# A transformer block with sparse attention, linear attention and 32 experts: the activation stage of the expert loop re-cut, and two steps of the loop put in another order

## The reference, cut to what matters

```python
def expert_block(xb, e):
    hgu = xb @ w_gate_up[e] + b_gate_up[e]          # 1024 -> 2048
    gate, up = jnp.split(hgu, 2, axis=-1)
    gate = jnp.minimum(gate, 7.0)
    up = jnp.clip(up, -7.0, 7.0)
    act = (up + 1.0) * (gate * jax.nn.sigmoid(1.702 * gate))
    return act @ w_down[e] + b_down[e]
```

## Time and profile before

| | us |
|---|---|
| median of 3 runs (1467.7, 1471.64, 1471.86) | 1471.64 |
| the profiled execution | 1467.8 |
| its span | 1466.0 |
| PE busy | 1378.1 (94%) |
| DVE busy | 498.9 (34%) |
| ACT busy | 249.7 (17%) |
| share of the chain that ended last: PE, DMA, SP's queue, ACT | 73%, 12%, 9%, 4% |
| bytes read | 482 MB |

### The profile page before, as it was taken

How to read it: one execution, slowest core, us unless ns; L and a number is a source line. 1 busy time by engine, 2 the same in 40 slices (tenths; PEclk the granted TensorE clock), 3 DMA queues, 4 the chain that set the end, 5 groups by cost and what they waited for, 6 DMA issues and landing times.

```text
span 1466.0 us, 17062 instructions
## 1 busy us (share of the span) xinstructions
PE 1378.1 (94%) x6275; PEld 619.7 (42%) x6276; DVE 498.9 (34%) x1032; ACT 249.7 (17%) x426; POOL 10.7 (1%) x35
## 2 busy tenths in 40 slices
PE   6999999999989999999999999999999999899996
PEld 3888455888443333333333333333333333223321
DVE  2250024556543233333333333323323323232233
ACT  3311025100011111111111111111111111111111
POOL 0000000000000000000000000000000000000000
PEclk9999999999969999999999999999999999999998
DMA  9734433899437639999699999979999999999994
GB/s 351 252 137 141 146 118 128 270 348 341 183 153 291 259 132 413 418 417 416 250 416 418 419 418 416 414 307 419 418 418 417 416 419 418 418 416 418 418 419 201
DMA packets 113088, 483.38 MB, mean 330 GB/s; under 512 B 10102, under 2 KB 10266, under 8 KB 80202
## 3 DMA queue, kind: packets, MB, share of 16 engines
q1 hardware_dynamic: 111666, 477.95, 81.9%
q0 software_dynamic: 1056, 4.06, 0.9%
q10 hardware_dynamic: 344, 1.07, 0.2%
HBM read 482.00 MB, written 1.05 MB: 329 GB/s over the span
## 4 chain that ended last, share of the span: by engine, by line
PE 73%; DMA 12%; SPq 9%; ACT 4%; issue 1%; DVE 1%; DVEq 0%; ACTq 0%
PE bank L1411 24%; PE bank L1100 14%; PE bank L1440 13%; DMA gu_slot<-in_w_gate_up 10%; PE bank L1109 8%; SPq L345 4%; SPq L350 4%; PE bank L1358 4%; PE bank L1390 3%; PE bank L1367 1%; ACT gx L633 1%; ACT xg L635 1%; ACT actT L637 1%; DMA piece<-in_w_ada 1%; DMA piece<-in_w_in 1%
## 5 line engine op out<-in xcount | busy, mean ns | idle before, releaser
L1411 PE MATMUL bank<-gu_slot,xg 128*64 128x512 f32 x2304 | 518.3, 597 | 18.6 <-DMA gu_slot<-in_w_gate_up 16.1
L1411 PEld LDWEIGHTS bank<-gu_slot,xg 128*64 128x64 f32 x2304 | 159.3, 137 | 365.8 <-issue 312.7
L1440 PE MATMUL bank<-dn_slot,actT 128*64 128x512 f32 x1152 | 255.1, 595 | 24.7 <-ACT actT L637 24.7
L1020 DVE TENSOR_TENSOR rowt<-bank,gt 128x512 f32<-128x512 f32 x144 | 92.8, 686 | 389.0 <-PE bank L1390 387.8
L1100 PE MATMUL bank<-hT,piece 128*128 128x256 f32 x704 | 155.2, 382 | 0.2 <-DMA piece<-in_w_in 0.2
L1440 PEld LDWEIGHTS bank<-dn_slot,actT 128*64 128x64 f32 x1152 | 79.4, 137 | 177.3 <-issue 144.0
L1100 PEld LDWEIGHTS bank<-hT,piece 128*128 128x128 f32 x704 | 134.5, 192 | 20.1 <-issue 1.1
L631 ACT ACTIVATE sig<-gcl 128x512 f32<-128x512 f32 x36 | 22.7, 630 | 571.4 <-DVE gcl L1038 571.4
L1038 DVE TENSOR_SCALAR gcl<-bank 128x512 f32<-128x512 f32 x36 | 24.9, 691 | 272.6 <-PE bank L1411 272.6
L1024 DVE TENSOR_TENSOR xs<-xs,rowt 128x512 f32<-128x512 f32 x144 | 93.1, 688 | 2.5
L1109 PE MATMUL bank<-piece,hT 128*128 128x512 f32 x192 | 83.2, 593 | 0.0
(11 more groups left out here) (279 smaller groups left out, 781.8 us busy)
## 6 DMA issues: line engine op xcount, KB each, us to landing
gu_slot<-in_w_gate_up SPq DMA_DIRECT2D x256, 1024.0 KB, 17.2
dn_slot<-in_w_down SPq DMA_DIRECT2D x128, 1024.0 KB, 17.2
piece<-in_w_in SPq DMA_DIRECT2D x17, 2048.0 KB, 8.8
piece<-in_w_ada SPq DMA_DIRECT2D x12, 2048.0 KB, 12.8
piece<-in_w_branch_a SPq DMA_DIRECT2D x2, 2048.0 KB, 8.5
piece<-in_w_branch_b SPq DMA_DIRECT2D x2, 2048.0 KB, 8.7
piece<-in_w_out SPq DMA_DIRECT2D x2, 2048.0 KB, 8.6
xs<-in_x ACTq DMA_DIRECT2D x1, 1024.0 KB, 8.9
```

The lines of the kernel that those rows point to most:

```text
L1020: ins = V.tensor_tensor(rowt[:, t, :], sum_bank[t][q][:], gt2[:, cols_], ALU.mult)
L1411: ins = M(bank[u][64 * q:64 * q + 64, :], xg[:, k % 4, 64 * (k // 4):64 * (k // 4) + 64], gu_slot[k][:, cols_], start=(k == 0), stop=(k == ...
L1440: ins = M(bank[5][64 * q:64 * q + 64, :], actT[:, f % 4, 64 * (f // 4):64 * (f // 4) + 64], dn_slot[f // 2][:, f % 2, 512 * q:512 * q + 51 ...
```

## The change

It does four things.

- The sigmoid reads gate from `bank[0]` itself, unclipped, as soon as the products are done (ACT waits for `gu_full`). DVE no longer writes a clipped gate ahead of it.
- gate's upper clip is done in two places: min(gate, 7) is formed inside the multiplication with the sigmoid, which now reads `bank[0]`, and the product is bounded from above by 7 sigmoid(1.702 x 7) (`GATE_MOST`), since above 7 the sigmoid of the unclipped gate is a little larger than that of the clipped one.
- The 1 added to up is added once to the biases, before they are cut into bf16 terms; up is clipped to -6 and 8 in place of -7 and 7.
- On PE the four transposes of the activations, with their waits, come before those of the gathered rows; on ACT the copy `actT` comes before `xg`.

```diff
+GATE_MOST = LIMIT / (1.0 + math.exp(-ALPHA * LIMIT))
 # ACT, per block
-                act.wait_ge(gcl_ready, g1_)
-                A(sig[:], gcl[:], ACT.Sigmoid, scale=ALPHA).then_inc(sig_ready, 1)
+                act.wait_ge(gu_full, g1_)
+                A(sig[:], bank[0][:], ACT.Sigmoid, scale=ALPHA).then_inc(sig_ready, 1)
                 act.wait_ge(gath_full, g2_)
                 A(gx[:], bank[2][:], ACT.Copy).then_inc(gx_out, 1)
+                act.wait_ge(actT_full, g1_)
+                A(actT[:].rearrange("p c s -> p (c s)"), bank[4][:], ACT.Copy).then_inc(actT_out, 1)
                 act.wait_ge(gxT_full, g2_)
                 A(xg[:].rearrange("p j s -> p (j s)"), bank[3][:], ACT.Copy).then_inc(xg_out, 1)
-                act.wait_ge(actT_full, g1_)
-                A(actT[:].rearrange("p c s -> p (c s)"), bank[4][:], ACT.Copy).then_inc(actT_out, 1)
 # DVE, once, before the loop
             dve.wait_ge(bgu_in, 48)
+            chain(V.tensor_scalar(bgu[:, D:2 * D], bgu[:, D:2 * D], 1.0, None, ALU.add))
             chain(V.tensor_copy(bias3[:], bgu[:]))
 # DVE, per block
                 dve.wait_ge(gu_full, g1_)
-                V.tensor_scalar(gcl[:], bank[0][:], LIMIT, None, ALU.min).then_inc(gcl_ready, 1)
-                V.tensor_scalar(ucl[:], bank[1][:], LIMIT, -LIMIT, ALU.min, ALU.max).then_inc(ucl_ready, 1)
+                V.tensor_scalar(ucl[:], bank[1][:], LIMIT + 1.0, 1.0 - LIMIT, ALU.min, ALU.max).then_inc(ucl_ready, 1)
                 dve.wait_ge(sig_ready, g1_)
-                V.tensor_tensor(gcl[:], gcl[:], sig[:], ALU.mult).then_inc(gs_ready, 1)
+                V.scalar_tensor_tensor(gcl[:], bank[0][:], LIMIT, sig[:], ALU.min, ALU.mult).then_inc(gs_ready, 1)
                 dve.wait_ge(gs_ready, g1_)
-                V.scalar_tensor_tensor(act_t[:], ucl[:], 1.0, gcl[:], ALU.add, ALU.mult).then_inc(act_ready, 1)
+                V.scalar_tensor_tensor(act_t[:], gcl[:], GATE_MOST, ucl[:], ALU.min, ALU.mult).then_inc(act_ready, 1)
 # PE, per block
-                pe.wait_ge(gx_out, g2_)
-                gather_transposes(bank[3])
                 pe.wait_ge(acc_out, g2_)
                 pe.wait_ge(act_ready, g1_)
                 for j in range(4):
                     ins = nc.tensor.transpose(bank[4][:, j * P:(j + 1) * P], act_t[:, j * P:(j + 1) * P], ident[:])
                 ins.then_inc(actT_full, 1)
+                pe.wait_ge(gx_out, g2_)
+                gather_transposes(bank[3])
                 pe.wait_ge(actT_out, g1_)
```

More of the change, by code:

```diff
@@ L1 @@
 import itertools
+import math
 from contextlib import ExitStack
```

## The result

| | before | changed |
|---|---|---|
| median, us (4 runs each) | 1470.37 | 1457.02 |
| lowest and highest, us | 1467.70, 1471.86 | 1456.55, 1459.95 |
| profiled execution, us | 1467.8 | 1456.55 |
| its span, us | 1466.0 | 1454.8 |
| from the first block's down products to the end, us | 1015.65 | 1006.84 |

The ratio is 0.9925 with a 95% interval of 0.9909 to 0.994: 0.6 to 0.9% faster, 9 to 13 us. A second measurement beside other runs of before gave 0.9932 (0.9918 to 0.9946). The two medians of the table lie 13.35 us apart, but four runs are few: over all runs on record, 53 of before and 10 of the changed kernel, the medians are 1468.34 and 1458.50 us, 9.8 us apart. The forecast said 1461 and a sum of 9.6 us.

What follows compares the result with a forecast made beforehand. PE and the expert loads were taken to bound the kernel in turn, so twelve of 36 stages at 0.80 us sum to 9.6 us: 1458.2 from the profiled execution, 1462.0 from the median, stated 1461; own range 1457 to 1464, 8-in-10 range 1456 to 1467.

Steps and rivals of the forecast that it cites:

- The path: Whole loop: PE and the loads set the pace in turn, so only twelve of 36 activation stages count.
- release of 708.11: SP may load the next expert after step k=0 of the present expert's last block; forecast to move to 700.1 us.
- (d): Expert loop: every one of the 36 stages counts, 28.8 us gained, 1442.8 us; chance 0.03.
- The stage: From DVE's first instruction to the down products: 4.27 us falls to 3.46, gain taken as 0.80 us.
- both halves of the change are needed: Activation stage: new order with old chain gains 0.08 us; old order loses the shorter act chain's gain.
- The slack of the first stretch: Loads ahead of PE before 700 us: slack 5.2 us, 4.0 of it spent, 1.2 remaining.
- about 1.5 us of room: Preparation, DVE's added 1 before PE's product ab3: cost nothing, or 0.75 us if the room were gone.
- the runs lie at two levels: Timed runs of the kernel before: 1467.7 to 1467.8 and 1471.6 to 1471.9 us; forecast set at 1461.
- own range: Whole kernel's time: 0.70 to 0.86 us per stage and either level of the runs, 1457 to 1464 us.
- (a): ACT's 1.28 us sigmoid table load moves behind the wait on gu_full: 5.9 us slower, 1477.5 us; chance 0.04.
- (b): ACT and DVE take turns at PSUM: stage gains 0.2 us, 2.4 us in all, 1469 us; chance 0.05.
- (c): Loads bound throughout and the dips are refilled: only the last stage counts, 1470.8 us; chance 0.06.

Runs made afterwards that it cites:

- halved loads: Kernel before and changed kernel, each loading only the gate half of every gate and up piece in the loop: 1446.61 and 1416.46 us, output not the reference's.
- the order alone: Kernel before with only the new order: act_t's transposes ahead of the gathered rows' on PE, actT ahead of xg on ACT: 1468.92 us, ratio 1.0003.
- the chain alone: Changed kernel with the old order on PE and ACT, keeping only the shorter elementwise chain: 1467.27 us, ratio 0.9995 to before.
- the halves: Changed kernel with DVE's product and act_t each cut into two halves of 256 columns: 1455.80 us, ratio 0.9908 to before; again 1454.59, 0.9906.

## Why the prediction was right, step by step

**The path.** PE-paced to the release of 708.11, loads to 943.5, one stage, loads to 1435.5, the last stage: twelve of 36. The changed profile has the same sequence, with the loads' distances 235.4 and 476.2 against the 235.5 and 476.6 forecast to stay. The release of 708.11 came at 698.92. With halved loads all stages count and the difference rose to 26.4 us, which is near what rival (d) put down for full loads, 28.8.

**The stage.** Forecast 3.46 us, measured 3.50; gain 0.77 rather than 0.80. The terms that were off: act_t ended at T+2.04 (forecast 2.08), since the sigmoid from PSUM took 0.60 and released DVE 0.03 later. PE took act_t 0.15 us after its end, where I had put 0.05, which is ACT's handover of gx. With the order alone it is 590.12 - 589.98 = 0.14 after 0.92 us of idle PE, so it is the handover and not PE being busy. The transposes of the gathered rows followed act_t's at 0.46 us (938.98 - 938.52) where I had put 0.59. Twelve stages make 9.2 us of the 9.6 forecast.

**What the profiles show beyond it.** The two spans differ by 11.2 us. 1.6 us of them lie before the first down products (2.39 less the one stage in it) and are scatter: SP's load at about 200 us, long before the first changed instruction, was already 1.16 us earlier (199.22 against 200.38), and over eleven profiles of the various versions the same load lies between 199.1 and 203.7. The other 0.46 us fall between that load and the loop; there the three profiles with the changed stage and the single added instruction, halved loads included, differ among each other by 0.50 us (248.74 to 249.24). Another 0.5 us came from the loads of sixteen experts, which took 475.9 to 477.1 us over nine profiles. Without these it is 9.1.

**That both halves of the change are needed** was argued from two chains 0.15 and 0.03 us apart, and the order alone and the chain alone show it: gains of 0.00 and 0.07 us per stage where 0.08 and 0 were put down.

**The slack of the first stretch.** Forecast 1.2 us left. In the changed kernel the DMA engines end that stretch at 692.1, as these two rows show (us, busy times, clock, DMA share, GB/s):

```profile
688.00:692.00 4.00, 3.60 (x22) 1.79 (x22) 1.85 (x7) 1.96 (x4) 0.00 (x0) 1.00 1.00 398
692.00:696.00 4.00, 4.00 (x22) 1.36 (x20) 0.00 (x0) 0.00 (x0) 0.00 (x0) 1.00 0.03 12
```

If the last gate and up piece landed 9.2 us earlier, as the forecast took from the other dip, it was there at 682.9; PE needed it at 689.87 - 5.49 = 684.4: an estimate of 1.5 us. The two profiles of the halves show that landing itself, 684.65 and 682.27, which is 145.65 and 145.78 us after the release at 539.00 and 536.49. By this distance the slack was 4.8 us in the kernel before (542.32 + 145.7 against 692.8), not 5.2, and is 1.0 in the changed one. The halves, with a stage 1.04 us shorter than before, should spend 5 x 1.04 = 5.2 us, 0.4 more than there is, and PE does wait there, 0.34 and 0.49 us.

**Where it was wrong.** "The product is two matmuls that ended at 312.3, so there is about 1.5 us of room": the idle time of DVE before 312.31 was put to the wrong product. The cost of the added instruction, 0.68 us on DVE and nothing at the end, was right by luck: the room was about 17 us, for a reason that the text did not have. And "the runs lie at two levels" was read out of four times; 49 later runs of before fill the range from 1466.2 to 1471.9 us. The middle that I took from them, 1461, was too high, and the measured 1457.0 lies at the lower edge of the own range of 1457 to 1464; from the profiled execution the sum gave 1458.2. The gain itself is off by less: 9.6 forecast, 9.8 between the medians of all runs.

**The rivals.** (a) is out: the table load stands at 425.29, 19 us ahead of the sigmoid, and in the stages shown the sigmoid starts at T. (b) is out: sigmoid and clip run side by side from T with 0.60 and 0.69 us. (c) is out: the dips are still there, and the nine periods before the first one became 6.81 us shorter. (d) is out: the spans differ by 11.2 us and not by 28.8. By an estimate from the Trainium skill, page "VectorE: DVE Perf Modes", section on the TRN2 errata, the product with a PSUM operand would have taken 0.065 us more than from SBUF; both took 0.69, so no run here shows that part. For ScalarE the same table of the Trainium skill gives 52 cycles less from PSUM, an estimate of 0.043 us; here it is 0.598 against 0.630 in the kernel before, 0.032 less.

## What to carry to other kernels

Look at a stage for a second chain of the same length before shortening the first: here the two edits are worth 0.00 and 0.07 us alone and 0.77 us together. Multiply a stage's gain by the blocks in which the engine sets the pace, read from where the loads stand still, not by all blocks. An idle time in a row names who ended it, but which result is needed there is in the code: count the rounds before calling it the room of a step.

## What the runs showed of the hardware that I had not expected

- PE takes a result of DVE 0.14 to 0.15 us after it ends, one of ACT 0.05 us (589.98 to 590.12 us with the order alone; 947.87 to 947.92 in the kernel before).
- ACT and DVE read two PSUM banks at the same time at full pace: 0.60 and 0.69 us, as each does by itself.
- The part before the loop scatters by up to 4.6 us from one execution to the next (199.1 to 203.7 us for the same load), nearly half of what the change brings, so the distance from the first down products to the end told the halves from the changed kernel better than their medians did.
